# The last pair of experts with the older second layer put first, and the last first layer summed in two other banks

## The reference

```python
def run_block(args):                       # for each expert e
    tok, e = args
    h = x_pad[tok] @ w1[e] + b1[e]         # 1024 -> 2048
    return clamped_swiglu(h) @ w2[e] + b2[e]   # 1024 -> 1024
...
y = y.reshape(P, D) * slot_g[:, None]      # times the gate
out = zeros.at[slot_tok].add(y)[:N]        # back to the tokens
return rms_norm(h + out, final_norm_w)
```

## Time and profile before

| | |
|---|---|
| median of 3 runs | 1287.34 us (1286.79 to 1288.43) |
| the profiled execution | 1288.56 us |
| its span, first to last instruction | 1286.3 us, 15495 instructions |
| PE busy, PE weight loads busy | 1211.1 us (94%), 591.9 us (46%) |
| DVE, ACT busy | 370.6 us (29%), 184.7 us (14%) |
| mean granted TensorE clock | 0.998 of full speed |
| moved by DMA | 449.26 MB, 349 GB/s over the span |
| chain that ended last, by engine | PE 63%, DMA 31%, DVE 4% |

### The profile page before, as it was taken

The page is one execution under the profiler, slowest core; times in us unless marked ns, Lnnn a source line. Parts: engine busy times, 40 slices in busy tenths (PEclk is TensorE's granted clock), DMA queues, the critical chain, the costliest instruction groups (busy, mean ns, idle before and its releaser), DMA issues.

```text
span 1286.3 us, 15495 instructions
## 1 busy us (share of the span) xinstructions
PE 1211.1 (94%) x6550; PEld 591.9 (46%) x6550; DVE 370.6 (29%) x629; ACT 184.7 (14%) x357; POOL 0.2 (0%) x4
## 2 busy tenths in 40 slices
PE   9999999999999999999998989898998989898986
PEld 7886788888543333333332323232333323232322
DVE  2158452411142233131331313122223313131223
ACT  2225521200120000100011000000010010100002
POOL 0000000000000000000000000000000000000000
PEclk9999999999999999999999999999999999999999
DMA  9354212695489999999999999999999999999995
GB/s 360 108 170 132 66 35 67 213 396 217 150 297 418 429 428 427 428 426 428 426 429 425 431 427 430 428 427 431 425 431 425 431 425 431 427 429 430 426 427 212
DMA packets 52131, 449.26 MB, mean 349 GB/s; under 512 B 5584, under 2 KB 18000, under 8 KB 26864
## 3 DMA queue, kind: packets, MB, share of 16 engines
q1 hardware_dynamic: 51744, 447.49, 84.3%
q10 hardware_dynamic: 336, 1.05, 0.3%
HBM read 447.48 MB, written 1.05 MB: 349 GB/s over the span
## 4 chain that ended last, share of the span: by engine, by line
PE 63%; DMA 31%; DVE 4%; issue 1%; ACT 1%; SPq 0%; DVEq 0%; PEldq 0%; ACTq 0%
PE ps L485 62%; DMA ring<-in_w_exp 19%; DMA upper<-in_w_exp 11%; PE ps L1021 1%; DVE ring L1485 1%; PE ps L746 0%; DMA xrows<-in_x 0%; DVE ring L1588 0%; DVE upper L1569 0%; ACT ring L1131 0%; DVE ring L1482 0%; PE ps L1032 0%; PE ps L652 0%; DVE upper L1524 0%; ACT upper L1197 0%
## 5 line engine op out<-in xcount | busy, mean ns | idle before, releaser
L485 PE MATMUL ps<-ring,upper 128*64 128x512 f32 (+4 forms) x2688 | 516.5, 527 | 30.6 <-DMA ring<-in_w_exp 26.3
L485 PE MATMUL ps<-upper 128*64 128x512 f32 (+5 forms) x1836 | 329.2, 461 | 23.4 <-DMA upper<-in_w_exp 15.8
L485 PEld LDWEIGHTS ps<-ring,upper 128*64 128x64 f32 (+2 forms) x2688 | 165.4, 136 | 340.3 <-issue 295.1
L485 PEld LDWEIGHTS ps<-upper 128*64 128x64 f32 (+3 forms) x1836 | 152.3, 154 | 191.4 <-issue 161.0
L485 PE MATMUL ps<-xT,ring 128*128 128x256 f32 x672 | 150.5, 381 | 0.4 <-DVE xT L1446 0.4
L485 PEld LDWEIGHTS ps<-xT,ring 128*128 128x128 f32 x672 | 126.1, 190 | 18.7 <-issue 1.1
L1752 DVE TENSOR_TENSOR upper<-ps,merged 128x512 f32<-128x512 f32 x32 | 22.1, 692 | 352.6 <-PEq L995 352.6
L1773 DVE TENSOR_TENSOR xrows<-xrows,ps 128x1024 f32<-128x1024 f32 x30 | 36.6, 1222 | 296.6 <-PE ps L485 296.6
L1349 ACT ACTIVATE xT<-upper 128x512 f32<-128x512 f32 x32 | 20.2, 631 | 544.9 <-DVE upper L1755 544.9
L1355 ACT ACTIVATE factors<-ps 64x512 f32<-64x512 f32 x63 | 37.3, 592 | 238.5 <-PEq L1016 237.7
L485 PE MATMUL ps<-factors,cst 128*128 128x512 f32 x128 | 63.2, 617 | 1.0 <-DVE factors L1832 1.0
(11 more groups left out here) (227 smaller groups left out, 491.8 us busy)
## 6 DMA issues: line engine op xcount, KB each, us to landing
ring<-in_w_exp SPq DMA_DIRECT2D x124, 2048.0 KB, 37.3
upper<-in_w_exp SPq DMA_DIRECT2D x63, 2048.0 KB, 37.3
ring<-in_w_exp SPq DMA_DIRECT2D x10, 1024.0 KB, 36.5
ring<-in_w_gate SPq DMA_DIRECT2D x9, 1024.0 KB, 5.2
ring<-in_w_in SPq DMA_DIRECT2D x8, 896.0 KB, 12.0
ring<-in_w_in SPq DMA_DIRECT2D x8, 640.0 KB, 4.0
ring<-in_w_branch SPq DMA_DIRECT2D x5, 1024.0 KB, 5.1
ring<-in_w_mem_kv SPq DMA_DIRECT2D x4, 1024.0 KB, 5.0
```

What stands on the lines that cost most here:

```text
L485: return pe.matmul(o, l, r, start=start, stop=stop, skip_group_check=True)
```

## The change

Twelve of the pieces at the end of the stream change places. The stream ends w2(29), w1(30), w1(31), w2(30), w2(31); its last 16 pieces are as before. PE follows: after turn(29) it does down(29), then up(30), then up(31), then down(30) and down(31). turn_gates(14) and both halves of scatter(14) move from up(31) into up(30), at the same piece numbers; turn(30) goes into up(31), after its piece 2. up(31) sums in banks 4 and 5, which `gather` uses in every earlier pair, and swiglu(31) reads them there. ACT does `downed(29)` and `gates_turned(14)` ahead of sigmoid(30), DVE both `add_up` of pair 14 ahead of swiglu(30). The loops of SP and PE lose their last turn, and experts 24 to 29 become straight code. No instruction of the computation is added or removed.

```diff
-        def w1_place(c, q, a, r, zero):
+        def w1_place(c, q, a, r, zero, swapped=False):
+            if swapped:
+                return place(q, a, r * CPE + c)
             return place(q, a, r * CPE + c if zero else r * CPE + c - 4)
...
-            return place(q, a, r * CPE + i + (8 if final else 16))
+            return place(q, a, r * CPE + i + (8 if final or swapped else 16))
...
+            def load_last_group(q):
+
+                for r in range(GROUP - 1):
+                    load_w1(q, GROUPS - 1, r + 1)
+                    load_w2(q, GROUPS - 1, r)
+                load_w2(q, GROUPS - 1, GROUP - 1, 4, False, True)
+                load_w1(q, GROUPS - 1, GROUP, False, False, True)
+
             def load_pass(q, very_first=False):
...
-                with sp.Fori(1 if very_first else 0, GROUPS) as a:
+                with sp.Fori(1 if very_first else 0, GROUPS - 1) as a:
                     load_group(q, a)
+                load_last_group(q)
                 load_w1(q, GROUPS, 1)
...
-                            last = mm(ps[64 * hf:64 * hf + 64, z, :], xg[:, c, parity * SLOTS:(parity + 1) * SLOTS],
+                            last = mm(ps[64 * hf:64 * hf + 64, bank + z, :], xg[:, c, parity * SLOTS:(parity + 1) * SLOTS],
...
+            def last_pair(q):
+
+                E, N = q * NE + NE - 2, q * NPAIR + NPAIR - 1
+
+                def scatters(c):
+                    if c == 0:
+                        turn_gates(N - 1, False)
+                    elif c == 2:
+                        scatter(N - 1, 0)
+                    elif c == 5:
+                        scatter(N - 1, 1)
+
+                def turn_even(c):
+                    if c == 2:
+                        turn(E)
+
+                def turn_odd(i):
+                    if i == 2:
+                        turn(E + 1)
+                        turn_gates(N, False)
+
+                down(q, GROUPS - 1, GROUP - 1, E - 1, 4, False, None, False, True)
+                pe.wait_ge(up_read, E)
+                up(q, GROUPS - 1, GROUP, E, N, 0, scatters, False, 0, True)
+                up(q, GROUPS, 1, E + 1, N, 1, turn_even, False, 4)
+                down(q, GROUPS, 0, E, 2, False, turn_odd)
+                down(q, GROUPS, 1, E + 1, 0, True)
+                scatter(N, 0, 6, True)
+                scatter(N, 1, 0, True)
...
-                with pe.Fori(1, GROUPS) as a:
+                with pe.Fori(1, GROUPS - 1) as a:
                     for p in range(GROUP // 2):
-                        pair(q, a, p, False, False)
-                pair(q, GROUPS, 0, False, True)
-                down(q, GROUPS, 1, q * NE + NE - 1, 0, True)
...
+                        pair(q, a, p, False)
+                for p in range(GROUP // 2):
+                    pair(q, GROUPS - 1, p, False)
+                last_pair(q)
...
+                if last:
+                    downed(E - 1, 1)
+                    gates_turned(N - 1)
                 sigmoid(E)
...
-            def swiglu(E, very_first=False):
+            def swiglu(E, very_first=False, bank=0):
...
-                TTn(glu, ps[:, 0, :], b1all[:, 0:D:2], ALU.add).then_inc(glu_raw, 1)
-                TTn(lin, ps[:, 1, :], b1all[:, 1:D:2], ALU.add).then_inc(up_read, 1)
+                TTn(glu, ps[:, bank, :], b1all[:, 0:D:2], ALU.add).then_inc(glu_raw, 1)
+                TTn(lin, ps[:, bank + 1, :], b1all[:, 1:D:2], ALU.add).then_inc(up_read, 1)
...
+                if last:
+                    add_up(N - 1, 0)
+                    add_up(N - 1, 1)
                 swiglu(E, very_first)
...
-                swiglu(E + 1)
+                swiglu(E + 1, False, 4 if last else 0)
```

More of the change, by code:

```diff
@@ L350, in place, with w2_place @@
             return s, q * per_pass[s] + a * TURNS + (m // RING + 1), q * PASS + a * (GROUP * CPE) + m
-        def w1_place(c, q, a, r, zero):
+        def w1_place(c, q, a, r, zero, swapped=False):
+            if swapped:
+                return place(q, a, r * CPE + c)
             return place(q, a, r * CPE + c if zero else r * CPE + c - 4)
-        def w2_place(i, q, a, r, final):
-            return place(q, a, r * CPE + i + (8 if final else 16))
+        def w2_place(i, q, a, r, final, swapped=False):
+            return place(q, a, r * CPE + i + (8 if final or swapped else 16))
         def odd_full(s, q):
@@ L422, in free, with load_w1 @@
                     sp.wait_ge(slots_used, n + (NMIX - RING))
-            def load_w1(q, a, r, zero=False, very_first=False):
+            def load_w1(q, a, r, zero=False, very_first=False, swapped=False):
                 for c in range(0, KC, 2):
-                    s, _, n = w1_place(c, q, a, r, zero)
+                    s, _, n = w1_place(c, q, a, r, zero, swapped)
                     free(n + 2, very_first)
@@ L432, in load_w1, with load_w2 @@
                       .then_inc(slot_full[s], 16)
-            def load_w2(q, a, r, whole=4, final=False):
+            def load_w2(q, a, r, whole=4, final=False, swapped=False):
                 for i in [*range(0, whole, 2), *range(whole, 4)]:
                     fine = i >= whole
-                    s, _, n = w2_place(i, q, a, r, final)
+                    s, _, n = w2_place(i, q, a, r, final, swapped)
                     free(n + (1 if fine else 2), False)
@@ L977, in gather, with up @@
                 last.then_inc(xg_ps, 1)
-            def up(q, a, r, E, N, parity, between, zero=False):
+            def up(q, a, r, E, N, parity, between, zero=False, bank=0, swapped=False):
                 for c in range(KC):
-                    s, times, n = w1_place(c, q, a, r, zero)
+                    s, times, n = w1_place(c, q, a, r, zero, swapped)
                     if parity == 0 and c % 4 == 0:
@@ L995, in up, with down @@
                 pe.sem_inc(up_ps, 1)
-            def down(q, a, r, E, whole=4, final=False, between=None, very_first=False):
+            def down(q, a, r, E, whole=4, final=False, between=None, very_first=False, swapped=False):
                 pe.wait_ge(actT_sb, E + 1)
@@ L1001, in down @@
                 for i in range(4):
-                    s, times, n = w2_place(i, q, a, r, final)
+                    s, times, n = w2_place(i, q, a, r, final, swapped)
                     if i % 2 == 0:
@@ L1056, in second_bias, with pair @@
                 last.then_inc(b2_ps, 1)
-            def pair(q, a, p, first, last, turn_wait=None):
+            def pair(q, a, p, first, turn_wait=None):
                 E, N, r = q * NE + a * GROUP + 2 * p, q * NPAIR + a * (GROUP // 2) + p, 2 * p
@@ L1086, in pair @@
                 up(q, a, r + 1, E + 1, N, 1, between)
-                def turns(i):
+                gather(N + 1)
+                down(q, a, r, E, 0 if very_first else 4, False, None, very_first)
+                turn(E + 1)
[12 more added lines that the diff above has]
+                def turn_odd(i):
                     if i == 2:
@@ L1104, in one_pass @@
                     gather(N0)
-                pair(q, 0, 0, True, False, "first" if very_first else None)
-                pair(q, 0, 1, False, False, "second" if very_first else None)
-                pair(q, 0, 2, False, False)
-                with pe.Fori(1, GROUPS) as a:
+                pair(q, 0, 0, True, "first" if very_first else None)
+                pair(q, 0, 1, False, "second" if very_first else None)
+                pair(q, 0, 2, False)
+                with pe.Fori(1, GROUPS - 1) as a:
                     for p in range(GROUP // 2):
-                        pair(q, a, p, False, False)
-                pair(q, GROUPS, 0, False, True)
-                down(q, GROUPS, 1, q * NE + NE - 1, 0, True)
-                scatter(N0 + NPAIR - 1, 0, 6, True)
-                scatter(N0 + NPAIR - 1, 1, 0, True)
+                        pair(q, a, p, False)
+                for p in range(GROUP // 2):
+                    pair(q, GROUPS - 1, p, False)
+                last_pair(q)
             one_pass(0, True)
@@ L1370, in pair @@
                     act.activation(gatesT[0:NE, :], ps[0:NE, 3, 0:T], ACT.Copy).then_inc(gT_sb, 1)
+                if last:
+                    downed(E - 1, 1)
+                    gates_turned(N - 1)
                 sigmoid(E)
-                if not first:
+                if not first and not last:
                     downed(E - 1, 1)
                 turned(E)
-                if not first:
+                if not first and not last:
                     gates_turned(N - 1)
```

## The result

The changed kernel takes 1291.57 us (median of 7 runs, 1289.82 to 1292.45) against 1287.34 (7 runs, 1286.79 to 1288.56): a ratio of 1.0027, 95% interval 1.0018 to 1.0036. The medians differ by 4.2 us, and the ratio stands for 3.5 us (2.3 to 4.6). It is slower, clear of the noise though by only a quarter of a percent, and the prediction (1287.5, range to 1289.4) was wrong. The profiled execution is the median one, 1291.57 us, with a span of 1289.8 against 1286.3.

A forecast was written before the change was run, and what follows sets the result against it. The prediction took the rate of the weight stream, 428 GB/s, as the bound. The median of 1287.34 us plus 0.2 for straight code and 0 for all other terms gave 1287.5 us, range 1285.6 to 1289.4.

The forecast's parts named there:

- the last landing plus the tail: End of the kernel: last weight piece lands at 1271.51 us, then a tail of 14.8 us to the span's end.
- the order's gain of 0: Last pair: PE reaches down(30) earlier, but still waits for the last piece, so the end gains 0.
- PE's times in the last pair: PE is 1.6 us earlier in up(31), waits before its last twin and down(30), and 0.7 us before the last piece.
- ACT's 1.1 us: Before down(29), PE must wait for ACT's copy, losing 1.1 us.
- turn(30) without a wait: In up(31), turn(30) finds its activations ready, with 2.1 us to spare; cost 0.
- the banks' 1.5 us: At up(31), banks 4 and 5 avoid a wait of some 1.5 us for DVE's reads; cost 0, gain 0 against before.
- SP's late issue: SP's last fine loads issue up to 1.7 us later, 9.6 us in hand: cost 0, up to 1.7 if landing followed issue.
- the one on straight code: Experts 24 to 29: fetching 5 or 6 more instruction packets, 0.09 MB, costs 0.2 us of the stream, bounds 0 to 1.
- C: Rival, slower by code: PE stops 2 us for each of six packets, about 1290 us; chance 0.04.
- A: Rival: PE bounds the end, so 4.4 us of scatters and gates moved out of up(31) come off, 1282.9 us; chance 0.04.
- B: Rival: a late turn(30) holds PE in up(31); beyond 4.6 us each microsecond counts, 1290.4 us; chance 0.04.
- D: Rival: PE isn't earlier at down(30), time the same, 1287.3 to 1287.5 us; chance 0.1 of the 0.88 for no change.

The follow-up runs named there:

- order_rolled: The change's order and banks in the first pass only, with SP's and PE's loops of four turns kept, against the kernel before: 1287.32 us, ratio 0.9995.
- code_pe: The kernel before with its order kept, only PE's last loop turn written out as straight code: 1290.46 us, ratio 1.0018.
- code_sp: The kernel before with its order kept, only SP's last loop turn written out as straight code, in both passes: 1289.81 us, ratio 1.0016.
- code_both: The kernel before with its order kept, the last turn of SP's and PE's loops written out as straight code: 1292.69 us, ratio 1.0035.

## Why the prediction was wrong

**That the end is the last landing plus the tail was right.** So were the order's gain of 0, PE's times in the last pair, ACT's 1.1 us (1.23), turn(30) without a wait, the banks' 1.5 us (1.48), SP's late issue without effect, and 6 q8 packets. Counted back from the last piece, up(31)'s last twin starts 19.7 us and down(30) 14.7 us ahead of it, where 19.6 and 14.7 were forecast; the wait before the last piece is 0.52 us, in order_rolled 0.67, for the 0.7 forecast.

**The step that failed is the one on straight code, twice.**

*The term was mis-sized.* It took 0.09 MB at 428 GB/s, 0.2 us, with a bound of 1 us taken from PE's idle time. This prices a packet of instructions by its bytes and spreads it over 16 engines. It lies on one, costs it 1.5 us, and the landing asks for the slowest. In the profiled executions the term is +0.54 us in the mean of the engines and +0.39 in the distance of the slowest, 0.93 us; a further 0.37 was there at 100 MB, before any changed code ran, which makes the 1.30 us of the landing. Of these the 0.54 us is firm (0.51 to 0.56 in three kernels); the 0.39 is within what this distance shows without more code (2.09 to 3.21). In the ratio code_pe puts longer PE code at 0.18% (0.09 to 0.27), 1.2 to 3.5 us, the first wait included. Six packets of 1.5 us are 0.6 us when dealt evenly over 16 engines and 9 us when all lie on the slowest: this, and not PE's idle time, should have been the bound.

*A term was missing.* The prediction counted code where it runs and not where it is jumped over. load_last_group stands in `load_pass`, which is also in the body of SP's `If`, so the body that SP skips at the very end grew. The branch was 0.52 us in the kernel before and 2.80 with the longer body, with nothing left to hide it: 2.3 us. code_sp alone gives 2.70 us there and a ratio of 1.0016, and taking the branch earlier takes most of it off the end. The prediction had the rule in hand, that of the Trainium skill, "Runtime: NRT & Kernel Launch", section "Instruction fetch mechanics", on a taken branch that leaves the window of fetched code, but applied it to PE's loop alone, as a possible gain. On SP's branch the runs agree with it: two body lengths, two prices, and with the higher price, in all three kernels that have it behind the stores, one more packet of instructions, 0.94 to 1.01 us after the branch. The records don't name the engine that a packet is for; that it is SP's follows from its time and from its absence where the branch takes 0.52 us.

*Of the rivals*, C (slower by code) had the right cause with the wrong mechanism: no wait of PE for its code shows. A, B and D didn't occur. The range ended at 1289.4 because the code was bounded by PE's idle time, and 0.88 for no change rested on that. Its sum doesn't come out either: 1287.5 with the spread of 1.1, the rest of the 1 us for code and the 1.7 for the issue, all of which it lists, is 1291.1. At the lower end the spread of 0.55, the 0.4 of PE and the 0.2 for code give 1286.35 and not 1285.6.

The sum for the spans, by rows: 0.37 (start) + 0.93 (landing) - 0.1 (from the slowest engine's end to SP's branch, 14.46 before, 14.36 after) + 2.3 (branch) = 3.5 us, 1289.8 - 1286.3.

## What to carry to other kernels

When a change unrolls a loop, list every queue on which the code grew, and on each the branches that jump over it, above all the last one of the program; a branch that must be taken at the end is best taken while the final stores are still on their way. In a stream that keeps all DMA engines busy, price a small extra transfer by the time of one engine and not by its bytes over the whole rate, because the last landing is that of the slowest engine. And test a bundled edit by its code alone before its idea: here the idea was worth nothing that could be measured, and its carrier cost 3.5 us.

## What the runs showed of the hardware

An instruction packet of 16 KB stops the weight packets of one DMA engine for 1.0 to 1.1 us, and the weight packet behind it takes 1.1 to 1.2 us instead of 0.61; in the saturated stream the lag of some 1.5 us stays (0.09 us per packet in the mean of the 16 engines' last ends). Behind the wait for the stores, SP's taken branch took 0.52 us to its drain without a packet of instructions of its own and 2.7 to 2.8 us with one. The engines' last weight packets end 5.2 us apart even in the kernel before (1265.84 to 1271.06), so a last piece of 1 MB, 2.45 us of the stream, waits mostly for the slowest engine. The Trainium skill, page "DMA: Bandwidth & Descriptors", section "Why a DMA increments its semaphore by 16 and not by 1", says that each engine counts its own share; the records agree, with the landing behind the slowest end. A copy of 17 rows (17 KB) took 9.85 us beside the stream, one of 16 rows 1.2 to 1.7 us. And the executions differ by up to 4 us when 100 MB have landed (457.68 to 461.76): PE sat idle 1.86 us near 8 us in code_both and 0.23 in the kernel before, and the granted clock was 0.66 in 9 to 14 us in the first and 1.00 in the second.
